# Input norm: weight and offset as rows spread by TensorE, first block's norm on VectorE alone, block 0 multiplied ahead of block 1's transposes

## Chip, core, metric

One core of a Trainium2 chip runs the whole program once. The metric is the device time of one execution in microseconds (us); several executions are summed up by their median. The engines are TensorE (PE, with its weight loads as PEld), VectorE (DVE), ScalarE (ACT), GpSimd (POOL) and SyncE (SP), which here only issues DMAs. Each engine runs its own program in order, and they wait for one another on semaphores.

## What is computed

One inference step of a decoder layer on 1024 prompt tokens and 64 sample tokens: an input layer norm, a combined projection that feeds sliding-window attention and a state-space mixer, an output projection, an MLP, and a gated embedding, each with a norm behind it. The change touches the start alone:

```
def layer_norm(x, g, b):
    mu = mean(x, -1); var = mean(square(x - mu), -1)
    return (x - mu) * rsqrt(var + LN_EPS) * g + b

hp, hs = layer_norm(x_prompt, ln_in_g, ln_in_b), layer_norm(x_sample, ln_in_g, ln_in_b)
...
proj = x @ w_in          # x is hp or hs: (tokens, 1024) @ (1024, 3080)
q, k, v, z, xbc, dt = split(proj)
...
```

## The kernel before

The tokens stand in NB = 9 blocks of 128 rows (the last has 64). In the function `stage_front` each block n passes through the same steps.

1. **Norm.** SP loads the block into X (three buffers). DVE's `statistics(n)` takes mean and variance (lines 109 to 112), POOL's `inverse_root(n)` makes 1/sqrt(var + eps) (lines 116, 118), DVE's `shift(n)` makes -mean/std (line 122), ACT's `normalise(n)` writes (x - mean)/std into H (line 127), POOL's `gain(n)` multiplies by the norm's weight G (line 132), and DVE's `add_bias(n)` adds the offset B (line 136) and raises `ln.done`. G and B are [128, 1024] tiles, each filled by a DMA that repeats one row of DRAM over 128 partitions.
2. **Transpose.** PE's `turn_x(n)` waits for `ln.done` and transposes the block in eight 128x128 pieces into PSUM (line 899; even blocks into fr_T, odd ones into fr_SS).
3. **Split.** ACT's `hi(n)` copies the transposed block to fp32r (line 732), DVE's `lo(n)` keeps the remainder (line 526). This pair stands in for an fp32 operand.
4. **Product.** PE's `tokens(n, 0)` multiplies the block by the first 344 columns of w_in for v and z: 24 matmuls (line 912; 8 pieces of the contraction times 3 hi/lo products). Those columns are split by ACT's `token_hi(0, k)` (line 736) and DVE's `token_lo(0, k)` (line 531), k = 0 to 7.

The order on each engine is written out by hand as a sequence of calls. On PE it is turn_x(0), turn_x(1), tokens(0), turn_x(2), tokens(1), turn_x(3), tokens(2), and so on: each product stands behind the transposes of the next block. On DVE add_bias(n + 1) stands behind lo(n), and on POOL inverse_root(n + 2) behind gain(n + 1). After the nine blocks come two more column groups of w_in and then 48 block products, all of which need every block's transposes; attention, projection and MLP follow as stages of their own.

Of the kernel before, what the change touches and what calls it, by code (L numbers as in the profile page):

```python
# [8 lines left out]
ALU = mybir.AluOpType  # L9
# [5 lines left out]
P = 128  # L15
# [143 lines left out]
def stage_front(nc, sem, io, ident, hT_hi, hT_lo, qT, kT, Xt, Bt, BT, CT, dt_raw, qk_start, xbc_start, top):  # L159
# [17 lines left out]
    X, H = norm("in_x", [P, 3, D]), norm("in_h", [P, 3, D])  # L177
    ln = LayerNorm(sem, norm, "in_ln")
    sb = lambda name, shape: top("sd_" + name, shape)
    tables = sb("tables", [P, sum(w for _, _, w in SSD_TABLES)])  # L180
    view, at = {}, 0
    for name, rows, width in SSD_TABLES:
# [27 lines left out]
             "xdt_done xdd_done masked e_done g_mm m_done y_mm o_mm off_done st_scaled y1_done s_mm st_done ss_low_scaled ss_high_scaled ss_done "  # L210
             "xsk_done y2_done y3_done z_loaded ssq_done ms_done rs_done yn_done st_out k_stored").split()
    S = {n: sem("fr_" + n) for n in names}
# [55 lines left out]
    with ExitStack() as ctx:  # L268
# [12 lines left out]
        def _(sp):  # L281
            def load_x(n):
                src = io["x_sample"] if n == NB - 1 else io["x_prompt"][n * P:(n + 1) * P, :]
                sp.dma_start(X[0:rows(n), n % 3, :], src).then_inc(x_loaded[n % 3], 16)
# [20 lines left out]

            load_x(0)
            sp.dma_start(ident[:, :], io["c_ident"]).then_inc(S["ident_loaded"], 16)
            sp.dma_start(ln.G[:, :], io["ln_in_g"].partition_broadcast(P)).then_inc(ln.loaded, 16)
            load_x(1)
            sp.dma_start(ln.B[:, :], io["ln_in_b"].partition_broadcast(P)).then_inc(ln.loaded, 16)  # L310
            load_token_weights(0)
# [100 lines left out]
        @block.gpsimd  # L412
        def _(pool):
            ln.constants(pool)

            def gain(n):
                r = rows(n)
                ln.gain(pool, H[0:r, n % 3, :], n % 2, n // 2, r)

            ln.inverse_root(pool, 0, 0, P)  # L420
            gain(0)
            ln.inverse_root(pool, 1, 0, P)
# [87 lines left out]
        def _(dve):  # L510
# [5 lines left out]
            def shift(n):  # L516
                ln.shift(dve, n % 2, n // 2, rows(n))

            def add_bias(n):
                ln.bias(dve, H[0:rows(n), n % 3, :], n % 2, n // 2, rows(n))  # L520
# [17 lines left out]
            statistics(0)  # L538
            shift(0)
            statistics(1)  # L540
            add_bias(0)
            shift(1)
            for k in range(KD // 2):
                token_lo(0, k)
            for n in range(NB):
                if n + 2 < NB:
                    statistics(n + 2)
                lo(n)
                if n == 0:
                    for k in range(KD // 2, KD):  # L550
                        token_lo(0, k)
                if n + 2 < NB:
                    shift(n + 2)
                if n + 1 < NB:
                    add_bias(n + 1)
# [165 lines left out]
        def _(act):  # L721
# [120 lines left out]

            normalise(0)
            for k in range(KD // 2):
                token_hi(0, k)
            normalise(1)
            for k in range(KD // 2, KD):
                token_hi(0, k)
            for n in range(NB):
                hi(n)  # L850
                if n + 2 < NB:
                    normalise(n + 2)
                if n >= 1:
                    evict_tokens(n - 1, 0)
                if 2 <= n < 6:
                    for k in range(2 * (n - 2), 2 * (n - 1)):
                        token_hi(1, k)
# [34 lines left out]
        def _(pe):  # L892
# [137 lines left out]

            pe.wait_ge(S["ident_loaded"], 16)
            turn_x(0)
            for n in range(NB):
                if n + 1 < NB:
                    turn_x(n + 1)
                tokens(n, 0)
# [1210 lines left out]
```

## Time and profile before

| what | value |
|---|---|
| median of 3 executions | 1626.64 us (1624.76 to 1627.03) |
| the profiled execution | 1625.73 us |
| its span, first to last instruction | 1623.9 us |
| PE busy | 1541.5 us, 95% of the span |
| DVE, ACT, POOL busy | 675.2, 489.1, 352.8 us |

The span is the time on the chip between the first and the last instruction that the trace shows; 1.8 us of the execution lie around it. Busy time says how long an engine had an instruction under way; matmuls overlap in their pipeline, so a busy PE need not be at its peak. Times in the trace's rows count from the start of the span.

### The profile page before, as it was taken

Reading aid. Unit: us, or ns where it says so; the run is one execution under the profiler, and the core shown is the slowest. Engines: PE = TensorE matmul, PEld = TensorE weight load, DVE = VectorE, ACT = ScalarE, POOL = GpSimd, SP = SyncE. Lnnn points to the kernel's source line nnn. Section 1 sums busy time; section 2 is a strip of 40 time slices with the busy share of each in tenths; the row PEclk is TensorE's granted clock in tenths of the full one; section 3 lists DMA queues with packets and bytes.
Section 4 is the critical chain, followed back from the end, with each engine's and each line's share of the span. In section 5 each row is a group of like instructions: output and inputs, shape, how many; then the busy total and the mean of one; then the engine's idle time right before and its main releaser. Section 6 shows DMA issues by size and latency. Waiting matters only on the chain.

```text
span 1623.9 us, 23323 instructions
## 1 busy us (share of the span) xinstructions
PE 1541.5 (95%) x9164; PEld 1343.1 (83%) x9164; DVE 675.2 (42%) x1233; ACT 489.1 (30%) x942; POOL 352.8 (22%) x375
## 2 busy tenths in 40 slices
PE   4999999998799989999999999999999999999997
PEld 4999998998365668798898989889898898977884
DVE  5412664552455655543232332323223232255655
ACT  4423223353456543342130302204021130323331
POOL 4300003463343522231010101101010010222442
PEclk9999999999899999999999999999999999999999
DMA  7531112441957221122030110202011020132011
GB/s 253 169 123 34 40 49 73 153 132 46 365 192 292 81 90 39 41 73 76 1 104 0 55 48 26 77 0 77 26 52 52 25 78 0 53 130 65 33 48 46
DMA packets 104655, 134.69 MB, mean 83 GB/s; under 512 B 6912, under 2 KB 78528, under 8 KB 104192
## 3 DMA queue, kind: packets, MB, share of 16 engines
q1 hardware_dynamic: 104576, 133.60, 24.6%
q8 instruction: 54, 0.88, 0.2%
q14 instruction: 25, 0.20, 0.0%
HBM read 113.25 MB, written 20.33 MB: 82 GB/s over the span
## 4 chain that ended last, share of the span: by engine, by line
PE 52%; issue 5%; DVE 3%; POOL 2%; DMA 1%; ACT 0%; SPq 0%; POOLq 0%; DVEq 0%; ACTq 0%
PE bk_U L1496 30%; PE bk_D L2016 18%; PE bk_D L1496 2%; POOL bk_u L1654 1%; PE bk_D L2011 1%; PE bk_D L2012 1%; DMA bk_wg_raw<-in_w_gate 1%; DVE bk_down_lo L1839 1%; DVE op_w_lo L1481 1%; DVE bk_m_lo L1823 1%; DVE R L1848 0%; PE bk_U L2048 0%; PE bk_D L1995 0%; POOL R L132 0%; DVE bk_wg_lo L1481 0%
## 5 line engine op out<-in xcount | busy, mean ns | idle before, releaser
L1496 PE MATMUL bk_U<-h1T_hi,bk_m_hi 128*128 128x364 f32 (+1 forms) x768 | 251.9, 328 | 4.8 <-PE bk_D L2016 4.8
L1496 PE MATMUL bk_U<-h1T_lo,bk_m_hi 128*128 128x364 f32 (+1 forms) x768 | 251.8, 328 | 0.0
L1496 PE MATMUL bk_U<-h1T_hi,bk_m_lo 128*128 128x364 f32 (+1 forms) x768 | 250.5, 326 | 0.0
L1654 POOL TENSOR_TENSOR bk_u<-bk_relu 128x364 f32<-128x364 f32 (+1 forms) x96 | 77.8, 811 | 639.9 <-ACT bk_relu L1701 639.8
L1701 ACT ACTIVATE bk_relu<-bk_U 128x364 f32<-128x364 f32 (+1 forms) x96 | 45.4, 473 | 554.4 <-PE bk_U L1496 554.4
L2016 PE MATMUL bk_D<-bk_down_hi,bk_u_hi 128*128 128x512 f32 x512 | 200.6, 392 | 6.5 <-DVE R L1848 3.1
L2016 PE MATMUL bk_D<-bk_down_lo,bk_u_hi 128*128 128x512 f32 x512 | 199.3, 389 | 0.0
L2016 PE MATMUL bk_D<-bk_down_hi,bk_u_lo 128*128 128x512 f32 x512 | 199.3, 389 | 0.0
L1848 DVE TENSOR_TENSOR R<-R,bk_D 128x512 f32<-128x512 f32 x144 | 98.5, 687 | 238.9 <-PE bk_D L2016 219.3
L1831 DVE TENSOR_TENSOR bk_u_lo<-bk_u,bk_u_hi 128x364 fp32r<-128x364 f32 (+1 forms) x96 | 50.9, 532 | 271.8 <-POOL bk_u L1654 271.8
L1496 PEld LDWEIGHTS bk_U<-h1T_hi,bk_m_hi 128*128 128x128 f32 x768 | 144.3, 188 | 7.8 <-issue 7.8
L1496 PEld LDWEIGHTS bk_U<-h1T_lo,bk_m_hi 128*128 128x128 f32 x768 | 144.4, 188 | 0.0
L1496 PEld LDWEIGHTS bk_U<-h1T_hi,bk_m_lo 128*128 128x128 f32 x768 | 144.1, 188 | 0.0
L923 PE MATMUL fr_mm<-hT_hi,fr_w_hi 128*128 128x364 f32 (+1 forms) x384 | 130.2, 339 | 0.0
L923 PE MATMUL fr_mm<-hT_hi,fr_w_lo 128*128 128x364 f32 (+1 forms) x384 | 126.5, 329 | 0.0
L923 PE MATMUL fr_mm<-hT_lo,fr_w_hi 128*128 128x364 f32 (+1 forms) x384 | 126.4, 329 | 0.0
L2016 PEld LDWEIGHTS bk_D<-bk_down_hi,bk_u_hi 128*128 128x128 f32 x512 | 96.1, 188 | 30.4 <-DVE bk_down_lo L1839 5.3
L2016 PEld LDWEIGHTS bk_D<-bk_down_hi,bk_u_lo 128*128 128x128 f32 x512 | 96.1, 188 | 20.1
L2016 PEld LDWEIGHTS bk_D<-bk_down_lo,bk_u_hi 128*128 128x128 f32 x512 | 96.1, 188 | 19.3
L1245 POOL TENSOR_TENSOR at_Z<-at_Z,at_inv 128x128 f32<-128x128 f32 (+7 forms) x64 | 72.1, 1147 | 101.8 <-DVE at_inv L1286 101.8
L923 PEld LDWEIGHTS fr_mm<-hT_hi,fr_w_hi 128*128 128x128 f32 x384 | 72.7, 189 | 1.1 <-issue 0.4
L923 PEld LDWEIGHTS fr_mm<-hT_lo,fr_w_hi 128*128 128x128 f32 x384 | 72.7, 189 | 0.2
(273 smaller groups left out, 2762.5 us busy)
## 6 DMA issues: line engine op xcount, KB each, us to landing
bk_up_raw<-in_w_up SPq DMA_DIRECT2D x32, 512.0 KB, 4.1
bk_down_raw<-in_w_down SPq DMA_DIRECT2D x32, 512.0 KB, 4.3
Kc<-in_cache_kT SPq DMA_DIRECT2D x8, 1536.0 KB, 13.5
Vc<-in_cache_v SPq DMA_DIRECT2D x8, 1536.0 KB, 9.8
fr_raw<-in_w_in SPq DMA_DIRECT2D x16, 512.0 KB, 4.0
in_x<-in_x_prompt SPq DMA_DIRECT2D x8, 512.0 KB, 6.2
h_scratch<-in_h SPq DMA_DIRECT2D x8, 512.0 KB, 3.2
sd_E<-acs_scratch SPq DMA_DIRECT2D x8, 512.0 KB, 3.8
```

What stands on the lines that cost most here:

```text
L923: last = pe.matmul(mm[:, u % 3, 0:w], wt[m % 2][:, k, :], ht[:, k, c:c + w], start=(k == 0 and part == 0), stop=(k == KD - 1 and part == 2))
L1245: pool.tensor_tensor(z, z, inv[:, m % NZ, u:u + 1].to_broadcast([P, n]), ALU.mult).then_inc(S["norm"], 1)
L1481: dve.tensor_tensor(self.lo[:, k, :], self.raw[:, k, :], self.hi[:, k, :].bitcast(F32), ALU.subtract).then_inc(self.lo_done, 1)
L1496: last = pe.matmul(out, a, b, start=(k == 0 and part == 0), stop=(k == n_k - 1 and part == 2))
L1654: pool.tensor_tensor(u[:, col:col + w], x, x, ALU.mult).then_inc(mul_done[g], 1)
L1701: act.activation(relu[:, col:col + w], pU[s][:, g, 0:w], ACT.Relu).then_inc(relu_done[s][g], 1)
L1823: dve.tensor_tensor(up_lo[s][:, :, :], up_raw[:, :, :], up_hi[s][:, :, :].bitcast(F32), ALU.subtract).then_inc(S["up_lo_done"], 1)
L1831: last = dve.tensor_tensor(u_lo[f][:, col:end], u[:, col:end], u_hi[f][:, col:end].bitcast(F32), ALU.subtract)
L1839: dve.tensor_tensor(down_lo[:, f, :], down_raw[:, :], down_hi[:, f, :].bitcast(F32), ALU.subtract).then_inc(S["down_lo_done"], 1)
L1848: dve.tensor_tensor(acc, acc, DD[:, s, :], ALU.add).then_inc(added[s], 1)
L2011: pe.matmul(out, both, down_hi[:, f, half], start=(f == 0), stop=False)
L2016: last = pe.matmul(out, a, b[:, f, half], start=(f == 0 and part == 0), stop=(f == FB - 1 and part == 2))
```

## The change

SP no longer fills G and B by DMA. It loads the two rows of 4 KB into partition 0 of H's third and second buffer (`g_row`, `b_row`), behind block 0 of X and ahead of `ident`. POOL sets a row of 128 ones. PE multiplies that row (as a 1x128 weight) with each half of the two rows, so that each of four matmuls with contraction 1 leaves 512 columns repeated over 128 partitions in PSUM, and ACT copies them to G and B.

Block 0's norm is `finish_first` on DVE: (x - mean) * G in one instruction and times 1/std plus B in a second, in place of shift, ACT's normalise, POOL's gain and add_bias. The order changes on PE (tokens(0) ahead of turn_x(1)), on ACT (hi(0) ahead of normalise(1)) and on DVE (below).

```diff
             load_x(0)
+            for row, src in ((g_row, io["ln_in_g"]), (b_row, io["ln_in_b"])):
+                sp.dma_start(row, src.rearrange("(a f) -> a f", a=1)).then_inc(S["rows_loaded"], 16)
             sp.dma_start(ident[:, :], io["c_ident"]).then_inc(S["ident_loaded"], 16)
-            sp.dma_start(ln.G[:, :], io["ln_in_g"].partition_broadcast(P)).then_inc(ln.loaded, 16)
             load_x(1)
-            sp.dma_start(ln.B[:, :], io["ln_in_b"].partition_broadcast(P)).then_inc(ln.loaded, 16)
...
             ln.inverse_root(pool, 0, 0, P)
-            gain(0)
             ln.inverse_root(pool, 1, 0, P)
...
+            def finish_first():
...
+                dve.wait_ge(ln.loaded, 32)
+                dve.wait_ge(ln.mv_done[0], 1)
+                dve.scalar_tensor_tensor(H[:, 0, :], X[:, 0, :], ln.mv[:, 0, 0:1], ln.G[:, :], ALU.subtract, ALU.mult)\
+                    .then_inc(ln.xn_done[0], 1)
+                dve.wait_ge(ln.xn_done[0], 1)
+                dve.wait_ge(ln.rstd_done[0], 1)
+                dve.scalar_tensor_tensor(H[:, 0, :], H[:, 0, :], ln.rstd[:, 0, :], ln.B[:, :], ALU.mult, ALU.add).then_inc(ln.done[0], 1)
...
             statistics(0)
-            shift(0)
+            finish_first()
             statistics(1)
-            add_bias(0)
             shift(1)
             for k in range(KD // 2):
                 token_lo(0, k)
-            for n in range(NB):
+            lo(0)
+            for k in range(KD // 2, KD):
+                token_lo(0, k)
+            add_bias(1)
+            statistics(2)
+            shift(2)
+            for n in range(1, NB):
...
-            normalise(0)
+            for v, (to, source) in enumerate(((ln.G, SS), (ln.B, mm))):
+                act.wait_ge(S["spread"], v + 1)
+                act.activation(to[:, :], source[:, 0:2, :].rearrange("p a b -> p (a b)"), ACT.Copy).then_inc(ln.loaded, 16)
...
             pe.wait_ge(S["ident_loaded"], 16)
+            pe.wait_ge(S["rows_loaded"], 32)
+            pe.wait_ge(S["one_set"], 1)
+            for to, row in ((SS, g_row), (mm, b_row)):
+                for half in range(2):
+                    last = pe.matmul(to[:, half, :], one[:, :], row[:, half * 512:(half + 1) * 512], start=True, stop=True)
+                last.then_inc(S["spread"], 1)
             turn_x(0)
-            for n in range(NB):
+            tokens(0, 0)
+            turn_x(1)
+            for n in range(1, NB):
                 if n + 1 < NB:
                     turn_x(n + 1)
                 tokens(n, 0)
```

On PE at the program's start, before (fr_T and fr_SS are the transposes' PSUM, fr_mm the products'; the seven further transposes of each block and, at the dots, block 0's further matmuls are left out):

```order
L899 MATMUL fr_T<-ident,in_h 128x128 [waits in_ln_done0,fr_ident_loaded]
L899 MATMUL fr_SS<-ident,in_h 128x128 [waits in_ln_done1]
L912 MATMUL fr_mm<-fr_t_hi_61,hT_hi 128x344 [waits fr_t_lo,fr_hT_lo_done]
...
L899 MATMUL fr_T<-ident,in_h 128x128 [waits fr_hT_lo_done,in_ln_done0]
L912 MATMUL fr_mm<-fr_t_hi_61,hT_hi 128x344 [waits fr_hT_lo_done]
```

And with the change, at the same place:

```order
L1057 MATMUL fr_SS<-in_h,in_one 128x512 [waits fr_one_set,fr_rows_loaded,fr_ident_loaded]
L1057 MATMUL fr_mm<-in_h,in_one 128x512 x2
L920 MATMUL fr_T<-ident,in_h 128x128 [waits in_ln_done0]
L933 MATMUL fr_mm<-fr_t_hi_61,hT_hi 128x344 [waits fr_t_lo,fr_hT_lo_done]
...
L920 MATMUL fr_SS<-ident,in_h 128x128 [waits in_ln_done1]
L920 MATMUL fr_T<-ident,in_h 128x128 [waits fr_hT_lo_done,in_ln_done0]
L933 MATMUL fr_mm<-fr_t_hi_61,hT_hi 128x344 [waits fr_hT_lo_done]
```

Block 0's product now stands between the transposes of blocks 0 and 1, and the transposes of block 2 follow at once on those of block 1.

On DVE, before, from the first split of the weights to block 2's offset:

```order
L531 TENSOR_TENSOR fr_t_lo_62<-fr_t_raw,fr_t_hi_61 128x344 [waits fr_t_hi_done] x4
L109 BN_STATS in_ln_bn<-in_x 128x6 [waits fr_x_loaded2]
...
L526 TENSOR_TENSOR hT_lo<-fr_T,hT_hi 128x8x128 [waits fr_hT_hi_done]
L531 TENSOR_TENSOR fr_t_lo_62<-fr_t_raw,fr_t_hi_61 128x344 [waits fr_t_hi_done] x4
L122 TENSOR_SCALAR in_ln_nmr<-in_ln_mv,in_ln_rstd 128x1 [waits in_ln_rstd_done0]
L136 TENSOR_TENSOR in_h<-in_h,in_ln_b 128x1024 [waits in_ln_gain_done1]
...
L526 TENSOR_TENSOR hT_lo<-fr_SS,hT_hi 128x8x128 [waits fr_hT_hi_done]
L122 TENSOR_SCALAR in_ln_nmr<-in_ln_mv,in_ln_rstd 128x1 [waits in_ln_rstd_done1]
L136 TENSOR_TENSOR in_h<-in_h,in_ln_b 128x1024 [waits in_ln_gain_done0]
```

And with the change:

```order
L546 TENSOR_TENSOR fr_t_lo_62<-fr_t_raw,fr_t_hi_61 128x344 [waits fr_t_hi_done] x4
L541 TENSOR_TENSOR hT_lo<-fr_T,hT_hi 128x8x128 [waits fr_hT_hi_done]
L546 TENSOR_TENSOR fr_t_lo_62<-fr_t_raw,fr_t_hi_61 128x344 [waits fr_t_hi_done] x4
L136 TENSOR_TENSOR in_h<-in_h,in_ln_b 128x1024 [waits in_ln_gain_done1]
L109 BN_STATS in_ln_bn<-in_x 128x6 [waits fr_x_loaded2]
...
L122 TENSOR_SCALAR in_ln_nmr<-in_ln_mv,in_ln_rstd 128x1 [waits in_ln_rstd_done0]
...
L541 TENSOR_TENSOR hT_lo<-fr_SS,hT_hi 128x8x128 [waits fr_hT_hi_done]
L122 TENSOR_SCALAR in_ln_nmr<-in_ln_mv,in_ln_rstd 128x1 [waits in_ln_rstd_done1]
L136 TENSOR_TENSOR in_h<-in_h,in_ln_b 128x1024 [waits in_ln_gain_done0]
```

Block 2's statistics have moved from ahead of block 0's split to behind block 1's offset.

On ACT the program now begins with these rows; before, the load of the activation table waited for nothing:

```order
L862 ACT_TABLE_LOAD [waits fr_spread]
L862 ACTIVATE in_ln_g<-fr_SS 128x1024
L862 ACTIVATE in_ln_b<-fr_mm 128x1024 [waits fr_spread]
L753 ACTIVATE fr_t_hi_61<-fr_t_raw 128x344 [waits fr_t_loaded0] x4
L749 ACTIVATE hT_hi<-fr_T 128x8x128 [waits fr_x_turned]
L127 ACTIVATE in_h<-in_x,in_ln_nmr,in_ln_rstd 128x1024 [waits in_ln_nmr_done1]
```

The table load has moved behind the first pair of spreading matmuls.

## Rows read from the trace of the kernel before

**Rows 1.** The page's first part: busy us, share of span, instructions.

```profile
PE 1541.5 (95%) x9164; PEld 1343.1 (83%) x9164; DVE 675.2 (42%) x1233; ACT 489.1 (30%) x942; POOL 352.8 (22%) x375
```

**Rows 2.** Windows: us; PE, PEld, DVE, ACT, POOL busy (instructions); granted clock; DMA share, GB/s.

```profile
0.00:16.00 16.00, 0.28 (x2) 0.31 (x3) 4.55 (x10) 4.15 (x6) 4.99 (x11) 1.00 0.79 282
71.00:76.00 5.00, 5.00 (x34) 5.00 (x33) 0.00 (x0) 1.91 (x3) 0.00 (x0) 1.00 1.05 305
```

**Rows 3.** Timeline, 0 to 16 us: start, us, instruction, [idle before <- releaser].

```profile
0.73 1.28 ACT L127 ACT_TABLE_LOAD   x1 [0.73 <-PEq L2235]
2.12 0.43 SPq L284 DMA_DIRECT2D in_x<-in_x_prompt  x1
4.32 0.69 DVE L109 BATCH_NORM_STATS2 in_ln_bn<-in_x 128x6 f32<-128x512 f32 x1 [4.32 <-DMA in_x<-in_x_prompt]
5.71 0.20 DVE L112 BATCH_NORM_AGGREGATE in_ln_mv<-in_ln_bn 128x2 f32<-128x12 f32 x1
6.91 0.21 DVE L122 TENSOR_SCALAR in_ln_nmr<-in_ln_mv,in_ln_rstd 128x1 f32<-128x1 f32 x1 [1.00 <-POOL in_ln_rstd L118]
11.97 2.34 POOL L132 TENSOR_TENSOR in_h<-in_h,in_ln_g 128x1024 f32<-128x1024 f32 x1 [5.10 <-DMA in_ln_b<-in_ln_in_b]
15.72 1.94 PE L899 MATMUL fr_T<-ident,in_h 128*128 128x128 f32 x8 [15.72 <-DVE in_h L136]
```

**Rows 4.** DMA issues, 0 to 20 us: KB each, median us to landing.

```profile
in_ln_g<-in_ln_in_g SPq DMA_DIRECT2D x1, 512.0 KB, 7.1
ident<-in_c_ident SPq DMA_DIRECT2D x1, 64.0 KB, 3.3
```

**Rows 5.** Timeline of PE, 24 to 36 us: transposes of blocks 1 to 3, block 0's first matmul.

```profile
24.20 1.97 PE L899 MATMUL fr_SS<-ident,in_h 128*128 128x128 f32 x8 [6.54 <-DVE in_h L136]
25.82 0.64 PE L912 MATMUL fr_mm<-fr_t_hi,hT_hi 128*128 128x344 f32 x1
31.10 1.03 PE L899 MATMUL fr_T<-ident,in_h 128*128 128x128 f32 x8
35.76 1.09 PE L899 MATMUL fr_SS<-ident,in_h 128*128 128x128 f32 x8
```

**Rows 6.** Timeline of DVE, ACT, POOL, 21 to 29 us: steps of blocks 1 and 2.

```profile
21.11 1.79 DVE L531 TENSOR_TENSOR fr_t_lo<-fr_t_raw,fr_t_hi 128x344 fp32r<-128x344 f32 x4
23.05 1.24 ACT L127 ACTIVATE in_h<-in_x,in_ln_nmr,in_ln_rstd 128x1024 f32<-128x1024 f32 x1 [3.12 <-DVE in_ln_nmr L122]
24.44 2.36 POOL L132 TENSOR_TENSOR in_h<-in_h,in_ln_g 128x1024 f32<-128x1024 f32 x1 [3.52 <-ACT in_h L127]
26.21 1.02 ACT L732 ACTIVATE hT_hi<-fr_SS 128x1024 fp32r<-128x1024 f32 x1 [1.91 <-PE fr_SS L899]
27.02 0.55 POOL L118 TENSOR_TENSOR in_ln_rstd<-in_ln_veps,in_ln_mhalf 128x1 f32<-128x1 f32 x1
27.27 1.23 DVE L526 TENSOR_TENSOR hT_lo<-fr_SS,hT_hi 128x1024 fp32r<-128x1024 f32 x1 [1.62 <-ACT hT_hi L732]
28.53 1.22 DVE L136 TENSOR_TENSOR in_h<-in_h,in_ln_b 128x1024 f32<-128x1024 f32 x1
```

**Rows 7.** Timeline of PE, later: plain fp32 matmuls of 256 columns, contraction 128 and 32.

```profile
292.52 1.08 PE L1006 MATMUL fr_SS<-sd_state,CT 128*128 128x256 f32 x4
277.71 6.09 PEld L1022 LDWEIGHTS fr_SS<-sd_xdd,sd_Bz 32*128 32x128 f32 x16 [0.39 <-DVE sd_state_s L676]
```

**Rows 8.** Groups by line on DVE, 1600 to 1624 us: last block's norm, first instruction.

```profile
L1927 DVE SCALAR_TENSOR_TENSOR bk_gate<-bk_gate,bk_ln_mv,bk_ln_g 64x1024 f32<-64x1024 f32 x1 | 1.3, 1270 | 0.0
```

**Rows 9.** Windows where the granted clock changes: columns as in rows 2.

```profile
397.50:398.00 0.50, 0.26 (x3) 0.02 (x1) 0.00 (x0) 0.50 (x2) 0.00 (x0) 1.00 0.00 0
401.00:401.50 0.50, 0.00 (x0) 0.00 (x0) 0.00 (x0) 0.00 (x0) 0.00 (x0) 0.52 1.06 386
278.00:279.00 1.00, 1.00 (x4) 0.79 (x4) 0.52 (x1) 0.00 (x0) 1.00 (x1) 0.57 0.00 1
280.00:281.00 1.00, 1.00 (x4) 0.76 (x3) 0.20 (x1) 0.00 (x0) 0.00 (x0) 0.50 0.00 0
```

More of the change, by code:

```diff
@@ L178, in stage_front @@
     ln = LayerNorm(sem, norm, "in_ln")
+    one = norm("in_one", [1, P])
+    g_row, b_row = H[0:1, 2, :], H[0:1, 1, :]
     sb = lambda name, shape: top("sd_" + name, shape)
@@ L210, in stage_front @@
              "xdt_done xdd_done masked e_done g_mm m_done y_mm o_mm off_done st_scaled y1_done s_mm st_done ss_low_scaled ss_high_scaled ss_done "
-             "xsk_done y2_done y3_done z_loaded ssq_done ms_done rs_done yn_done st_out k_stored").split()
+             "rows_loaded one_set spread xsk_done y2_done y3_done z_loaded ssq_done ms_done rs_done yn_done st_out k_stored").split()
     S = {n: sem("fr_" + n) for n in names}
@@ L413, in _ @@
         def _(pool):
+            pool.memset(one[:, :], 1.0).then_inc(S["one_set"], 1)
             ln.constants(pool)
@@ L517, in shift @@
                 ln.shift(dve, n % 2, n // 2, rows(n))
+            def finish_first():
[6 more added lines that the diff above has]
+                dve.scalar_tensor_tensor(H[:, 0, :], H[:, 0, :], ln.rstd[:, 0, :], ln.B[:, :], ALU.mult, ALU.add).then_inc(ln.done[0], 1)
+                dve.sem_inc(ln.nmr_done[0], 1)
+                dve.sem_inc(ln.gain_done[0], 1)
             def add_bias(n):
@@ L548, in _ @@
                 lo(n)
-                if n == 0:
-                    for k in range(KD // 2, KD):
-                        token_lo(0, k)
                 if n + 2 < NB:
@@ L841, in read_turned @@
                 last.then_inc(S["uev"], 1)
-            normalise(0)
+            for v, (to, source) in enumerate(((ln.G, SS), (ln.B, mm))):
+                act.wait_ge(S["spread"], v + 1)
+                act.activation(to[:, :], source[:, 0:2, :].rearrange("p a b -> p (a b)"), ACT.Copy).then_inc(ln.loaded, 16)
             for k in range(KD // 2):
                 token_hi(0, k)
+            hi(0)
             normalise(1)
@@ L849, in _ @@
             for n in range(NB):
-                hi(n)
+                if n >= 1:
+                    hi(n)
                 if n + 2 < NB:
```

## The prediction, made blind

> **What bounds the kernel now.** I read the page's busy shares first, then the windows of the start, then the timeline of each engine there. The shares say that PE is the engine to look at: busy 95% of the span [rows 1]. The windows say where it is not: in the first 16 us PE works 0.28 us, and from some point on it works without a gap (5.00 of 5 us at 71 us) [rows 2]. In between, PE begins block 0's transposes at 15.72 us, block 1's at 24.20, block 0's product at 25.82 [rows 3, 5], and the rest follows closely. So the front is worth what it moves PE's later work. I measure that at one point: the start of block 3's transposes, 35.76 us [rows 5]. In both programs PE has by then done the transposes of blocks 0 to 2 and the products of blocks 0 and 1, and what follows has the same order.
>
> What holds the first 15.72 us? Block 0's statistics begin when X lands, at 4.32, and end at 5.91; 1/std is there 1.00 us later [rows 3]. Then POOL's gain sits idle 5.10 us, until 11.97, for the landing of B, which is a DMA of 512 KB; gain takes 2.34 and the offset 1.2 more [rows 3, 6]. That wait is what the change goes after. The second idle stretch, up to 24.20, ends with block 1's offset on DVE [rows 5].
>
> **Part 1: when block 0's norm is done (T0).** The rows of G and B are small, and `ident`, which PE also waits for, is now fourth in SP's queue, where X of block 1 was issued at 2.12; with its 3.3 us to land it is there at 5.4 [rows 3, 4]. Bounds: 4.5 if it lands as early as before (two places earlier in the queue, which takes some 0.45 us a place), 8.8 if the second row, issued where G was (about 1.65), takes the 7.1 us that G took [rows 4]. I take 5.4: a row of 4 KB is nearer to ident's 64 KB than to G's 512.
>
> No row shows a matmul with contraction 1 and 512 columns in fp32. The nearest are fp32 with 256 columns: four in 1.08 us at contraction 128, 0.27 each, and 16 weight loads (one to a matmul) in 6.09 us at contraction 32, 0.38 each, the latter while the granted clock stood at 0.50 [rows 7, 9]. PE comes out of idleness here, and block 0's and 1's transposes (1.94, 1.97) take twice those of blocks 2 and 3 (1.03, 1.09) [rows 3, 5], so I price at the half clock: 512 columns between 2 x 0.38 = 0.76 and 4 x 0.27 = 1.08; I take 0.85, nearer to the row of small contraction. The first pair ends at 5.4 + 1.7 + 0.2 of pipeline = 7.3, the second at 9.0.
>
> ACT's table load takes 1.28 us; before it ran at 0.73, under the load of X [rows 3], and now the first pair's wait stands ahead of it, so that cover is gone: 8.6. Each copy out of PSUM is priced as ACT's 1.02 for the same size [rows 6]: G at 9.65, B at 10.7. The two DVE instructions of `finish_first` are like the last block's, 1.27 each [rows 8]: T0 = 13.3. Before, it was 15.7, PE's start. So this part gives 2.4 us. Bounds from the above: 12.1 (all low) to 16.7 (rows landing at 8.8).
>
> The Trainium skill, page "FP8 and Floating Point Precision", section "TensorE Precision Notes", says that true fp32 takes four passes through the array. The trace does not bear it out: 0.27 us for 256 columns is 2.5 times the 0.107 of one pass at 2.4 GHz. By the page each spreading matmul would cost about 1.7 us, the second pair would end at 12.4, and T0 would be 16.0.
>
> Costed at nothing: 1 MB less to load (X of block 1 and the weights come earlier, but DVE reads block 1 only after T0, and ACT the weights after the copies), POOL's memset of 128 ones (it ends under the load of X), POOL's gain of block 0 (POOL has nothing else to do then). The load of X for block 3 now waits for `finish_first`'s first half, at 12; its reader comes at T0 + 11 = 24, and 7 us to land [rows 4] fit.
>
> **Part 2: from T0 to block 2's offset.** Here DVE's order is the matter. After T0 one chain runs through DVE, POOL and ACT, each step priced from a row: block 1's statistics 1.6, 1/std 1.0, shift 0.1 [rows 3]; four weight splits at 1.7 (they start to start in 1.79 less overlap), block 0's `lo` 1.2, four more splits 1.7, block 1's offset 1.15 [rows 6]: T0 + 8.5. Only then block 2's statistics, 1/std and shift, 2.7: T0 + 11.2. Then ACT's normalise 1.24 and POOL's gain and, queued behind gain, block 3's 1/std: in the trace from 23.05 to 27.57, 4.5 us [rows 6]. DVE's shift of block 3 waits for that 1/std, and block 2's offset (1.22) stands behind the shift: T0 + 17.2.
>
> PE in that time: transposes of block 0 at T0, product at T0 + 5.7 = 19.0, when `lo` is done. Before, that product ran from 25.82 to 31.10, 5.28 us [rows 5]; now until 24.3, and block 1's transposes until some 25.5 to 26.5. Block 1's own path (ACT's hi 1.02, lo 1.23) ends before POOL's chain and costs nothing. But PE's next instruction is block 2's transposes, at T0 + 17.2 = 30.5. Nothing stands between: **PE waits 4 to 5 us**, where before block 0's product filled that place. So the product starts 6.8 us earlier and most of it is given back in one stall; block 2's transposes start at 30.5 against 31.10 [rows 5].
>
> **Part 3: the clock.** Out of a warm stretch, block 2's transposes and block 1's product take 35.76 - 31.10 = 4.66 us; the same work out of idleness took 31.10 - 24.20 = 6.90 (blocks 1 and 0) [rows 5]. So 2.24 us hang on whether the granted clock falls from 2.4 to 1.2 GHz in the stall. PE's last work before attention is at 397.8, and the clock falls between 401.0 and 401.5; it also falls in a stretch of matmuls with contraction 32, at which PE is busy throughout [rows 9]. A stall of 4 to 5 us is longer than those 3.5, so I take the fall as likelier. The windows give a clock of 1.00 for the first 16 us too [rows 2], where the transposes take the time of the half clock; at the start I go by the durations.
>
> The Trainium skill, page "TensorE: Matmul & The Clock Gate", section "HAM oscillation — how this bites in real kernels", speaks against this change: idle gaps between groups of matmuls put the clock back, and each group starts slow. By that rule the stall costs its idle time and the 2.24 us.
>
> **Sum.** 30.5 + 6.90 = 37.4 against 35.76: +1.6 us. On the profiled execution's 1625.73 that is 1627.4. The median of the runs shown is 0.9 above that execution; I add half of it: **1627.8 us**.
>
> **Rivals.**
> - *The clock holds through the stall* (PE stopped for less than at 397.8, or the fall comes too late to matter): 30.5 + 4.66 = 35.2, -0.6: 1625.1. For it: the fall at 401 took 3.5 us of full idleness, and the stall may be shorter.
> - *The spread is late* (slower). The rows land as late as G did, which puts T0 at 16.7, or the spreading matmuls take twice the time priced, which puts it at 16.0. Everything hangs on T0, so the point moves by 2.7 to 3.4 more: +4.3 to +5.0, 1630.0 to 1630.7. It decides from T0 = 14.9 on (+3.25 in all). Against it: ident's 3.3 us and the rows of 256 columns.
> - *The stall does not come* (faster): block 2's offset is ready when PE wants it, PE goes on from block 0's product at 24.3 through block 1's transposes (1.03) and 4.66 more: 30.0, -5.8: 1619.9. For it: PE's first product does start 6.8 us earlier. Against it: the order of DVE and POOL, by which block 2's statistics come after block 1's offset; all 17.2 us of the chain are priced from rows, and 6 us of them would have to vanish.
> - *Nothing moves:* would need T0 at 13.9 with the clock held, or near 11.7 with the fall; it lies inside the range.
>
> **Numbers.** About 0.2%, 3.25 us, is what a measurement of this kernel can tell from no change. The forecast has 0.55, the clock that holds 0.25; both lie within 0.2%. The late spread has 0.13 (slower; 0.08 by late rows, 0.05 by dear matmuls), the missing stall 0.07 (faster). The range leaves these last two out: low 1625.1 less the 1.2 of T0's low bound, 1623.9; high 1627.4 with T0 at 14.9 (+1.6) and the whole 0.9 of the median, 1629.9.
>
> **What would show it.** Right: G's copy waiting for a table load after the first spread; the second instruction of `finish_first` ending near 13.3; block 0's product starting near 19; PE idle 4 to 5 us before block 2's transposes with DVE's offset as releaser, and block 2's transposes at 1.9 us rather than 1.0 behind it; block 3's transposes at 37.4. Wrong: T0 beyond 15 (rows or spreading matmuls dearer than priced), no stall there, or a difference that arises after 40 us, where I expect none.

## The result, and the profile after

| | before | after |
|---|---|---|
| median of 11 executions each, us | 1627.03 (1624.41 to 1629.83) | 1633.01 (1630.11 to 1634.1) |
| ratio of the times | | 1.0034, 95% interval 1.0026 to 1.0042 |
| the profiled execution, us | 1625.73 | 1633.81 |
| block 0's transposes start | 15.72 | 16.25 |
| block 2's transposes start | 31.10 | 34.32 |
| block 3's transposes start | 35.76 | 40.56 |
| block 8's transposes start (the last) | 60.22 | 65.04 |

The kernel is slower by 0.34%, some 6 us. The prediction said 1627.8 us, no change that can be told (0.80), slower with 0.13; the time lies outside its range, 1623.9 to 1629.9. First the top of the page, against [rows 1]:

```profile
span 1632.0 us, 23348 instructions
...
PE 1553.9 (95%) x9172; PEld 1349.9 (83%) x9172; DVE 677.6 (42%) x1233; ACT 489.4 (30%) x943; POOL 349.8 (21%) x375
```

PE is busy 12.4 us longer; the eight records of the spread are 7.2 us of that (5.24 to 12.43). The timeline of the changed kernel up to 17 us answers to [rows 3]:

```profile
5.24 3.78 PE L1057 MATMUL fr_SS<-in_h,in_one 1*128 1x512 f32 x4 [5.24 <-DMA ident<-in_c_ident]
...
8.81 3.62 PE L1057 MATMUL fr_mm<-in_h,in_one 1*128 1x512 f32 x4
9.10 1.28 ACT L862 ACT_TABLE_LOAD   x1 [9.10 <-PE fr_SS L1057]
10.40 1.02 ACT L862 ACTIVATE in_ln_g<-fr_SS 128x1024 f32<-128x1024 f32 x1
12.53 1.02 ACT L862 ACTIVATE in_ln_b<-fr_mm 128x1024 f32<-128x1024 f32 x1 [1.11 <-PE fr_mm L1057]
...
13.59 1.28 DVE L526 SCALAR_TENSOR_TENSOR in_h<-in_x,in_ln_mv,in_ln_g 128x1024 f32<-128x1024 f32 x1 [7.51 <-ACT in_ln_b L862]
...
14.91 1.28 DVE L530 SCALAR_TENSOR_TENSOR in_h<-in_h,in_ln_rstd,in_ln_b 128x1024 f32<-128x1024 f32 x1
```

The rows and `ident` are there at 5.24, as forecast. But the program issues two spreading matmuls for a row, and the trace has four records for it (x4), 0.85 us each: the first row is spread at 9.1, the second at 12.4. The table load, the copies and the two DVE instructions follow at their forecast lengths, and block 0's norm is done at 16.2.

PE from there on, against [rows 5]:

```profile
16.25 1.97 PE L920 MATMUL fr_T<-ident,in_h 128*128 128x128 f32 x8 [3.82 <-DVE in_h L530]
21.73 0.66 PE L933 MATMUL fr_mm<-fr_t_hi,hT_hi 128*128 128x344 f32 x1 [3.52 <-DVE hT_lo L541]
...
28.15 1.04 PE L920 MATMUL fr_SS<-ident,in_h 128*128 128x128 f32 x8
...
34.32 1.97 PE L920 MATMUL fr_T<-ident,in_h 128*128 128x128 f32 x8 [5.13 <-DVE in_h L136]
...
40.56 1.03 PE L920 MATMUL fr_SS<-ident,in_h 128*128 128x128 f32 x8
```

Block 0's product does start early (21.73 against 25.82), and PE then stands 5.13 us for block 2's offset. Block 3's transposes are 4.80 late, block 8's 4.82: from there on nothing is won back or lost in the front.

The windows of the changed kernel (us; busy of PE, PEld, DVE, ACT, POOL; granted clock) at the stall and in the tail:

```profile
33.50:34.00 0.50, 0.00 (x0) 0.00 (x0) 0.50 (x1) 0.50 (x1) 0.00 (x0) 1.00 0.05 16
34.00:34.50 0.50, 0.18 (x1) 0.19 (x2) 0.50 (x2) 0.50 (x2) 0.00 (x0) 0.68 0.00 0
34.50:37.50 3.00, 3.00 (x13) 3.00 (x13) 1.35 (x5) 1.35 (x2) 2.79 (x3) 0.50 0.83 266
...
1454.00:1458.00 4.00, 4.00 (x12) 3.13 (x11) 1.16 (x2) 3.95 (x4) 2.39 (x1) 0.57 0.00 0
...
1488.00:1492.00 4.00, 4.00 (x12) 3.17 (x11) 1.52 (x2) 2.31 (x3) 0.00 (x0) 0.57 0.99 320
```

Before, at the same times (the same work lies 5 to 7 us earlier there, where the clock reads 1.00 too):

```profile
1452.00:1458.00 6.00, 6.00 (x28) 4.96 (x27) 3.93 (x8) 1.02 (x2) 1.24 (x3) 1.00 0.00 0
1488.00:1492.00 4.00, 4.00 (x19) 3.24 (x18) 0.00 (x0) 0.00 (x0) 0.00 (x0) 1.00 0.07 20
```

And PE's first matmuls behind its two pauses in that part of the tail, before (the first two) and after:

```profile
1448.27 0.50 PE L2016 MATMUL bk_D<-bk_down_hi,bk_u_hi 128*128 128x512 f32 x1 [1.81 <-DVE R L1848]
1481.09 0.47 PE L1496 MATMUL bk_U<-bk_wg_hi,bk_m_hi 128*128 128x512 f32 x1 [3.14 <-DVE bk_wg_lo L1481]
...
1453.20 0.50 PE L2045 MATMUL bk_D<-bk_down_hi,bk_u_hi 128*128 128x512 f32 x1 [1.81 <-DVE R L1877]
1487.64 0.47 PE L1525 MATMUL bk_U<-bk_wg_hi,bk_m_hi 128*128 128x512 f32 x1 [3.14 <-DVE bk_wg_lo L1510]
```

The granted clock falls to 1.2 GHz (0.50) as PE comes out of the stall. In the tail it falls twice more, behind pauses of PE of 1.81 and 3.14 us; before has the same two pauses, and its clock stays at 1.00. These two falls make the difference of the two spans 8.1 us instead of 4.8 to 5.1. They come and go from one execution to the next: of the 14 profiles of this case, 6 have the first fall (after, e2, e3, e6, e9, e10) and 13 the second, all but this first one of before (see `before_again` below). So I read a kernel's front at block 8's transposes, and its time from the medians.

### The profile page after: what moved, and what is told of

Its sections match the earlier page's. It is cut to its first block, busy times and chain, and to the rows that moved or that the text cites. A ratio compares the mean times of both kernels' runs of the same rounds, so it can differ in the third digit from the quotient of the medians.

```text
span 1632.0 us, 23348 instructions
## 1 busy us (share of the span) xinstructions
PE 1553.9 (95%) x9172; PEld 1349.9 (83%) x9172; DVE 677.6 (42%) x1233; ACT 489.4 (30%) x943; POOL 349.8 (21%) x375
## 4 chain that ended last, share of the span: by engine, by line
PE 52%; issue 5%; DVE 3%; POOL 2%; DMA 1%; ACT 0%; SPq 0%; POOLq 0%; DVEq 0%; ACTq 0%
PE bk_U L1525 30%; PE bk_D L2045 18%; PE bk_D L1525 2%; POOL bk_u L1683 1%; PE bk_D L2040 1%; PE bk_D L2041 1%; DMA bk_wg_raw<-in_w_gate 1%; DVE bk_down_lo L1868 1%; DVE op_w_lo L1510 1%; DVE bk_m_lo L1852 1%; DVE R L1877 0%; PE bk_U L2077 0%; PE bk_D L2024 0%; POOL R L132 0%; DVE bk_wg_lo L1510 0%
## 5 line engine op out<-in xcount | busy, mean ns | idle before, releaser
L933 PE MATMUL fr_mm<-fr_t_hi,hT_hi 128*128 128x344 f32 (+1 forms) x216 | 71.3, 330 | 3.5 <-DVE hT_lo L541 3.5
## 6 DMA issues: line engine op xcount, KB each, us to landing
Kc<-in_cache_kT SPq DMA_DIRECT2D x8, 1536.0 KB, 13.3
```

Of the source, the lines that this page charges most:

```text
L933: last = pe.matmul(mm[0:r, u % 3, 0:TOKEN_GROUP], ht[:, k, to], wt[g][:, k, :], start=(k == 0 and part == 0), stop=(k == KD - 1 and part = ...
```

## The experiments

Starts of PE's transposes, us, from one profile each. T0 is the start of block 0's.

| kernel | T0 | block 2 | block 3 | block 8 | block 8 against before | ratio of times (95%) |
|---|---|---|---|---|---|---|
| before | 15.72 | 31.10 | 35.76 | 60.22 | | |
| after | 16.25 | 34.32 | 40.56 | 65.04 | +4.82 | 1.0034 (1.0026 to 1.0042) |
| e1_norm_only | 15.82 | 32.54 | 37.21 | 61.71 | +1.49 | 1.0020 (1.0011 to 1.0030) |
| e2_order_only | 15.48 | 33.52 | 39.52 | 63.99 | +3.77 | 1.0035 (1.0021 to 1.0049) |
| e5_half_spread | 13.20 | 31.25 | 38.13 | 62.55 | +2.33 | 1.0026 (1.0015 to 1.0037) |
| e3_psum_direct | 13.37 | 31.90 | 38.37 | 62.80 | +2.58 | 1.0024 (1.0015 to 1.0033) |
| e9_no_gain1 | 16.43 | 33.31 | 39.55 | 64.01 | +3.79 | one execution |
| e4_stats2_early | 15.78 | 29.13 | 37.84 | 63.68 | +3.46 | 1.0025 (1.0014 to 1.0035) |
| e6_block1_early | 13.99 | 31.18 | 36.09 | 60.54 | +0.32 | 1.0005 (0.9995 to 1.0014) |
| e8_norm_old_loads | 14.71 | 30.06 | 34.72 | 59.18 | -1.04 | 0.9995 (0.9986 to 1.0004) |
| e10_norms_first | 12.46 | 26.79 | 32.60 | 61.62 | +1.40 | 1.0025 (1.0016 to 1.0035) |
| e11_spread_norms_first | 13.55 | 27.12 | 32.93 | 61.95 | +1.73 | 1.0027 (1.0017 to 1.0036) |
| e12_norms_first_old_loop | 13.25 | 28.46 | 33.37 | 57.83 | -2.39 | 0.9981 (0.9972 to 0.9990) |

**The two parts apart: e1_norm_only and e2_order_only.** e1 puts before's order back into the changed kernel, but for one thing: `finish_first` still stands ahead of block 1's statistics on DVE. e2 puts the new order alone into before.

```diff
 e1, PE, against after (DVE and ACT likewise; e2, against before, the reverse)
             turn_x(0)
-            tokens(0, 0)
-            turn_x(1)
-            for n in range(1, NB):
+            for n in range(NB):
```

> The changed kernel with the order of before on VectorE, ScalarE and TensorE; the rows, their spread by TensorE and the two instructions of finish_first stay. Theory A (the loss is the dear spread plus the order): block 0's norm is done at 16.2 as in the changed kernel (15.7 before), block 1's statistics come behind it, so block 1's transposes start near 26.8 (24.20 before), block 2's near 33.7 (31.10), block 3's near 38.4 (35.76), with no stall over 1 us ahead of block 2's transposes and the clock held from there on; the whole is 2.6 us slower than before and some 2 us faster than the changed kernel. Rival B (the loss arises after 40 us, in stages where the clock falls): the total does not follow block 3's transposes, and this kernel is as slow as the changed one (+5.5 us) though its point is 2 us earlier.

> The kernel before with its loads and its norm of block 0 left as they are (shift, normalise, gain, offset), and only the new order of instructions on VectorE, ScalarE and TensorE. Theory A: block 0's norm is done at 15.7 as before; block 1's statistics are out of the way by then, so block 2's offset comes at some 32.5 (16.8 behind block 0's); TensorE stands idle for 5 to 6 us between block 1's and block 2's transposes, the granted clock falls to about 0.5 there, and block 3's transposes start 6.2 later, near 38.7: +2.9 against before, with nothing of the spread in it. Rival C (the order is harmless, the whole loss is the spread's lateness): block 3's transposes at 35.8 or earlier, no stall, and the time as before within 1 us.

e1's block 8 is +1.49, e2's +3.77; together 5.26, about the changed kernel's 4.82. Both parts lose, and the order loses more, without any spread in it. e1's T0 is within 0.1 us of before's; what it loses comes behind T0. Block 1's statistics, which before has done by 12.2, start at 15.68, behind `finish_first`, and block 1's transposes start at 26.38 instead of 24.20. In e2 PE:

```profile
24.98 1.09 PE L904 MATMUL fr_SS<-ident,in_h 128*128 128x128 f32 x8
33.52 1.97 PE L904 MATMUL fr_T<-ident,in_h 128*128 128x128 f32 x8 [7.45 <-DVE in_h L136]
```

The wait for block 2's offset is 7.45 us, longer than forecast: T0 to block 2 took 18.0, not 16.8. Rival C (the order is harmless) falls. Rival B (the whole loss arises after 40 us) falls with e1: its time is between the two kernels', as its front is. That nothing is lost after 40 us does not follow: e2's time is some 5.7 us above before's (1.0035), its front 3.77.

**Was the matmul's price the wrong step? e5_half_spread and e3_psum_direct.** e5 issues one matmul for a row (ACT's copy puts that half into both), and its spread then costs what I had priced. e3 leaves out the wait for ACT's table load and copies instead.

```diff
 e5
-                for half in range(2):
-                    last = pe.matmul(to[:, half, :], one[:, :], row[:, half * 512:(half + 1) * 512], ...)
+                last = pe.matmul(to[:, 0, :], one[:, :], row[:, 0:512], ...)
 e3, finish_first (offset likewise, from mm)
-                dve.wait_ge(ln.loaded, 32)
+                dve.wait_ge(S["spread"], 1)
-                ... ln.mv[:, 0, 0:1], ln.G[:, :], ALU.subtract, ALU.mult)
+                ... ln.mv[:, 0, 0:1], flat_pair(SS), ALU.subtract, ALU.mult)
```

> The changed kernel with one spreading matmul for each row in place of two: only the first 512 numbers of weight and offset are spread, and the copy puts them into both halves, so the columns from 512 on get other weights and offsets than the reference's. One matmul (two records of 0.85) then takes what the prediction priced for two. Theory A (the price of the spreading matmul is the step of the sum that failed, the rest of the sum stands): the first spread is done near 7.2, block 0's norm at 13.3, block 2's transposes at 30.5 to 31.4, block 3's at 37.4 (prediction) to 37.7, and the time 1.6 to 2 us above before. Rival (block 0's norm is held by something else, the landing of the rows or X, not by the spread): block 0's norm at 16, block 3's transposes at 40.5 as in the changed kernel.

> The changed kernel, but the two instructions of finish_first read weight and offset straight from PSUM; ScalarE copies them out for the later blocks only after VectorE has read them. Theory A (the spread holds block 0's norm, and what follows is a chain of fixed length behind it): the second spread is done at 12.3, so block 0's norm at 13.6 to 13.9 (16.2 in the changed kernel), block 2's transposes 18.1 later, near 31.9, with a stall of 5 to 6 us ahead of them; block 8's transposes near 62.7 (65.04 in the changed kernel, 60.22 before); the time 2.5 to 4 us above before. Rival (an instruction that reads PSUM is dearer, or the later copies hold ScalarE's weight splits up, so that nothing is won): block 8's transposes at 64 or later.

e5's timeline:

```profile
5.11 2.07 PE L1056 MATMUL fr_SS<-in_h,in_one 1*128 1x512 f32 x2 [5.11 <-DMA ident<-in_c_ident]
...
13.20 1.97 PE L920 MATMUL fr_T<-ident,in_h 128*128 128x128 f32 x8 [4.31 <-DVE in_h L530]
...
31.25 1.97 PE L920 MATMUL fr_T<-ident,in_h 128*128 128x128 f32 x8 [6.05 <-DVE in_h L136]
...
38.13 1.03 PE L920 MATMUL fr_SS<-ident,in_h 128*128 128x128 f32 x8
```

One matmul, two records (x2). With the price that I had assumed, block 0's norm is done at 13.2 (prediction 13.3), block 3's transposes start at 38.1 (37.4), and the kernel is still slower than before. The 0.7 that is left at block 3 lies between T0 and block 2 (18.05 instead of 17.2; next experiment). The time misses its forecast of 1.6 to 2 us above before: it is some 4.2 us above (1.0026), the front 2.33. e3 comes within 0.3 us of its forecast at each start (13.37, 31.90, 62.80), though its stall is 6.71, not 5 to 6. So the spread's price shifts T0, what follows shifts with it, and the stall came at every T0 measured with this order (13.20 to 16.43).

**The shared wait of VectorE and GpSimd: e9_no_gain1.** The chain from T0 to block 2's transposes took 18.1 us in the changed kernel, not 17.2. Its timeline:

```profile
18.75 1.79 DVE L546 TENSOR_TENSOR fr_t_lo<-fr_t_raw,fr_t_hi 128x344 fp32r<-128x344 f32 x4
...
20.55 2.36 POOL L132 TENSOR_TENSOR in_h<-in_h,in_ln_g 128x1024 f32<-128x1024 f32 x1 [1.96 <-ACT in_h L127]
21.59 2.97 DVE L546 TENSOR_TENSOR fr_t_lo<-fr_t_raw,fr_t_hi 128x344 fp32r<-128x344 f32 x4
24.49 1.21 DVE L136 TENSOR_TENSOR in_h<-in_h,in_ln_b 128x1024 f32<-128x1024 f32 x1
```

The second group of four weight splits takes 2.97 where the first takes 1.79, and runs beside POOL's gain. e9 leaves out that gain:

```diff
             def gain(n):
+                if n == 1:
+                    ...
+                    pool.sem_inc(ln.gain_done[1], 1)
+                    return
```

> The changed kernel without GpSimd's gain of block 1 (its rows leave the norm without the weight). Theory D (the 2.97 us that the second group of weight splits takes, 1.2 more than the first, is time in which VectorE stands while GpSimd's gain runs): that group takes 1.8, block 1's offset starts near 23.3 instead of 24.49, block 2's transposes 1.2 earlier, near 33.1, block 8's near 63.9. Rival (the group waits for ScalarE's splits or for something else): it still takes 3 us, and block 2's transposes stay at 34.3.

e9's rows of the same steps:

```profile
21.77 1.79 DVE L551 TENSOR_TENSOR fr_t_lo<-fr_t_raw,fr_t_hi 128x344 fp32r<-128x344 f32 x4
23.47 1.22 DVE L136 TENSOR_TENSOR in_h<-in_h,in_ln_b 128x1024 f32<-128x1024 f32 x1
```

The group takes 1.79 again, and the chain is 16.9 (33.31 - 16.43), 1.2 less. So DVE stood while the gain ran.

**Taking the stall away: e4_stats2_early.** Block 2's norm is started earlier (on POOL its 1/std goes ahead of block 1's gain):

```diff
 e4, DVE, against after
             statistics(1)
+            statistics(2)
             shift(1)
 ...
             lo(0)
+            shift(2)
 ...
             add_bias(1)
-            statistics(2)
-            shift(2)
+            add_bias(2)
```

> The changed kernel with block 2's statistics right behind block 1's, its 1/std ahead of block 1's gain on GpSimd, its shift behind block 0's lo and its offset right behind block 1's offset. Theory A: block 0's norm is done at 16.2 as in the changed kernel, block 2's offset is done before TensorE has finished block 1's transposes, so the stall of 5.1 us is gone or under 1.5 us, the clock does not fall, and block 3's transposes start near 36.1 (40.56 in the changed kernel, 35.76 before): the time is that of before within 1 us, 4 to 5 us less than the changed kernel's. Rival B (the loss arises after 40 us): the time stays about 5 us above before. Rival D (VectorE and GpSimd hold each other up at SBUF, so that earlier work of block 2 only takes longer): single instructions of 1.7 to 2.4 us instead of 0.5 to 1.2 on VectorE while GpSimd's gain runs, and block 3's transposes after 38.

The stall ahead of block 2 is gone, as forecast, but 36.1 for block 3 was missed by 1.7, and the front is still +3.46. The time was forecast within 1 us of before's and is some 4 us above it (1.0025). e4's timeline:

```profile
21.63 4.90 DVE L547 TENSOR_TENSOR fr_t_lo<-fr_t_raw,fr_t_hi 128x344 fp32r<-128x344 f32 x4
...
29.13 1.04 PE L922 MATMUL fr_T<-ident,in_h 128*128 128x128 f32 x8
31.66 0.43 PE L935 MATMUL fr_mm<-fr_t_hi,hT_hi 128*128 128x344 f32 x1 [1.50 <-DVE hT_lo L542]
...
37.84 1.93 PE L922 MATMUL fr_SS<-ident,in_h 128*128 128x128 f32 x8 [2.12 <-DVE in_h L136]
```

Two gains now run beside the splits, which take 4.90 us; all later steps of DVE slide, and PE waits in two other places, for lo of block 1 and for block 3's offset (2.12, at which the clock falls: 1.93 us for the transposes). Rival D had the larger part of this. A stall taken away at one block came back, shorter, at the next.

**Better orders: e8, e6, e10, e11, e12.** e8 keeps before's loads and order and takes only the norm on VectorE, behind block 1's statistics; e6 spreads the rows as e3 does and moves block 1's norm ahead of the end of block 0's, with before's order on PE (the diff shows the main lines; ACT's copies and normalise move in e6 too).

```diff
 e8, DVE, against before
             statistics(0)
-            shift(0)
             statistics(1)
-            add_bias(0)
+            finish_first()
             shift(1)
 e6, DVE, against after
             statistics(0)
-            finish_first()
             statistics(1)
             shift(1)
+            finish_first()
+            statistics(2)
             ...
```

> The kernel before with one part of the change alone: block 0's norm on VectorE by finish_first, behind block 1's statistics; weight and offset are loaded spread out by DMA as before, and every order is that of before. Theory A: the landing of the offset (11.97 before) still releases it, but two VectorE instructions (2.5 us) follow in place of gain and offset (3.7), so block 0's norm is done near 14.6 (15.6 before), 1/std of block 1 is no longer queued behind block 0's gain, block 1's transposes start near 23.0 (24.20), block 3's near 34.6 (35.76), block 8's near 59.0 (60.22): 1 to 1.5 us faster than before. Rival (the norm on VectorE is itself a loss, since VectorE is the engine that every block waits for): block 8's transposes at 60.2 or later.

> Rows, spread and finish_first from PSUM as in e3_psum_direct, TensorE's order as before (block 1's transposes ahead of block 0's product), and block 1's statistics, 1/std, shift and normalise put ahead of block 0's end, into the time in which the spread is awaited; block 2's statistics come right behind finish_first. Theory A (what counts is the chain of norms on VectorE, GpSimd and ScalarE, and the wait for the spread is room for block 1's part of it): block 0's norm is done at 13.9, block 1's near 18.5, TensorE has block 0's product from 20.5 on, no stall over 1 us ahead of block 2's transposes, block 3's transposes between 30.4 and 32 (35.76 before) and block 8's near 55 to 56.5 (60.22 before): 4 to 5 us faster than before. Rival D (VectorE's instructions with two SBUF inputs stand while GpSimd's gain runs): the weight splits take 3 to 5 us a group instead of 1.8, block 3's transposes at 33 to 34, 2 us faster at most.

e8's front came as forecast at each point (14.71, 23.20, 34.72, 59.18): with DMA-spread rows the norm on VectorE gains 1.04 us. That is too little for the times to show (0.9995). In e6 the splits stood beside a gain once more (3.67 us), and that gain waited until 17.08 for ACT's copy of the offset. Its forecast failed: block 1's transposes start at 22.27 (18.5 forecast), block 3's at 36.09 (30.4 to 32, and 33 to 34 by rival D), and it is as fast as before instead of 4 to 5 us faster.

e10 splits finish_first, so that its first half waits for the weight alone, and puts all norm steps ahead of the weight splits; e11 is the same with the spread of e3.

```diff
             statistics(0)
+            finish_first()       # (x - mean) * G
             statistics(1)
+            finish_second()      # * 1/std + B
             shift(1)
+            statistics(2)
+            lo(0)
+            add_bias(1)
+            shift(2)
             (8 splits)
             for n in range(1, NB):
                 statistics(n + 2)
-                lo(n)
-                shift(n + 2)
                 add_bias(n + 1)
+                shift(n + 2)
+                lo(n)
```

> The loads of before; block 0's norm on VectorE as in e8_norm_old_loads, but its first instruction waits for the weight alone and goes ahead of block 1's statistics; behind it VectorE and ScalarE do what the next norms wait for first (statistics of block 2, offset of block 1, shift of block 2), and the weight splits after that; later blocks take the offset ahead of the lo of the block before. TensorE's order is that of before. Theory A and D together (the chain of norms sets the front; weight splits beside a running gain only stand): block 0's norm is done near 13.4, block 1's transposes start near 19, block 0's product near 21 with no stall over 1 us behind it, block 3's transposes near 32.2 (35.76 before), block 8's near 56.6 (60.22): 3 to 4 us faster than before. Rival (the norms are not the bound, VectorE's whole work is): block 8's transposes at 59 as in e8_norm_old_loads, or later, with VectorE busy without a gap from 14 to 30.

> The same order with the rows spread by TensorE and read from PSUM as in e3_psum_direct. Theory A: the second spread is done at 12.3, where the offset of before lands at 12.0, so block 0's norm is done near 13.5, as in e10_norms_first; ScalarE's copies for the later blocks put block 1's gain 0.6 to 1 us later, and block 8's transposes come within 1 us behind those of e10_norms_first, near 57.2, 3 us ahead of before. Rival (the rows are worth something that the order hid): 1 us or more ahead of e10_norms_first. Rival (the copies cost ScalarE what the weight splits and hi of block 0 need): 2 us or more behind it.

Up to block 3 e10 is where it was forecast (32.60, 3.2 ahead of before). Then it loses 0.88 us at each block, 5.81 where before takes 4.93. Its DVE:

```profile
32.98 0.21 DVE L122 TENSOR_SCALAR in_ln_nmr<-in_ln_mv,in_ln_rstd 128x1 f32<-128x1 f32 x1 [0.43 <-POOL in_ln_rstd L118]
33.11 1.21 DVE L542 TENSOR_TENSOR hT_lo<-fr_T,hT_hi 128x1024 fp32r<-128x1024 f32 x1
```

lo(2) stands behind a shift that waits for POOL, while PE, done with block 3's transposes (32.60), waits for lo(2), 0.69 us at each block. My loop, not the idea, was wrong. The rival's number (59 or later) came true, its reason did not: DVE is busy 12.8 of the 16 us from 14 to 30. e11 runs 0.33 us behind e10 from block 2 on, as forecast; spread or loaded rows come to the same within the 0.8 us by which the landing of the weight differs between two executions (below). Its block 8 fails with e10's loop. e12 puts the loop of before back:

```diff
                 statistics(n + 2)
+                lo(n)
+                shift(n + 2)
                 add_bias(n + 1)
-                shift(n + 2)
-                lo(n)
```

> e10_norms_first with one thing put back: from block 1 on, VectorE takes lo of the block ahead of the shift and the offset of the next ones, as the kernel before does. Theory A, with what e10_norms_first showed (its front was early, block 3's transposes at 32.60, but each later block took 5.81 us instead of 4.93, because lo stood behind a shift that waits for 1/std): block 2's transposes start near 27.6, block 3's near 32.4 and each block behind takes 4.93 us again, so block 8's start near 57.0 (60.22 before) and the time is some 3 us below that of before, a ratio near 0.998. Rival (the early front leaves block 3 or 4 without its norm, and a stall of 2 to 4 us comes there): block 8's transposes at 59 or later, as in e8_norm_old_loads.

e12's PE:

```profile
13.25 1.94 PE L915 MATMUL fr_T<-ident,in_h 128*128 128x128 f32 x8 [13.25 <-DVE in_h L531]
20.53 1.97 PE L915 MATMUL fr_SS<-ident,in_h 128*128 128x128 f32 x8 [5.34 <-DVE in_h L136]
28.46 1.10 PE L915 MATMUL fr_T<-ident,in_h 128*128 128x128 f32 x8 [0.72 <-DVE in_h L136]
33.37 1.09 PE L915 MATMUL fr_SS<-ident,in_h 128*128 128x128 f32 x8
```

Stall 0.72, blocks 4.9 apart again, block 8 at 57.83. All points lie 0.8 to 1.0 behind those forecast: in this execution the weight landed at 9.07, in e10's at 8.26, and T0 moved with it. The median is 1624.58 against 1628.10 in the same comparison: 0.9981 (0.9972 to 0.9990), faster than both kernels. That is 3.5 us for a front of 2.39; where the rest comes from is not shown, and the profiled execution (1627.82) is the slowest of its eleven.

**The tail: before_again**, the kernel before unchanged.

> The kernel before, unchanged, profiled once more. If the two short falls of the granted clock near 1450 and 1485 us, which the changed kernel's execution shows and the first one of before does not, belong to the execution and not to the change, an execution of before can show one or both as well, and is then 1.5 to 3 us longer than the first (span 1623.9) with the same front (block 3's transposes at 35.8, block 8's at 60.2). If they come of the change, this execution has none and its span is within 0.5 us of 1623.9.

Its front is 0.38 us earlier than in the first profile, its span 2.5 longer, and it has a window of which the first profile has none like it:

```profile
1480.00:1486.00 6.00, 3.97 (x11) 3.15 (x12) 2.85 (x3) 2.05 (x3) 0.00 (x0) 0.72 0.99 309
```

So the second fall belongs to the execution and not to the change. The first one is in 6 profiles of 14, e6's among them, whose front is within 0.4 us of before's; that it too comes by execution is likely, but no kernel was profiled both with it and without.

## Why the prediction was wrong, point by point

- **Rows and `ident` at 5.4:** right (5.24). Rival "late rows" did not happen.
- **The price of a spreading matmul, 0.85:** this is the step that failed, and T0 at 16.25 is beyond the 15 that I named as a sign of it. I read [rows 7]'s "x4 in 1.08" as four matmuls. The program has 16 matmuls on that line; the trace of before answers for it, over the whole span:

```profile
L1006 PE MATMUL fr_SS<-sd_state,CT x32: 379/379/435, 292.5 to 383.7; 128*128 128x256 f32 x32
...
L1022 PEld LDWEIGHTS fr_SS<-sd_xdd,sd_Bz x32: 181/185/332, 273.8 to 283.5; 32*128 32x128 f32 x32
```

Thirty-two records, two for each matmul, and as many weight loads for the 16 matmuls of line 1022: by the same reckoning 256 columns cost 0.54 us, not 0.27, and the bounds for 512 columns were 1.52 to 2.16 us, twice my 0.76 to 1.08. A spreading matmul takes 2 x 0.855 = 1.71 us, between them: the reckoning was right, its unit wrong. Of T0's 2.9 us too much (16.2 for 13.3), 1.8 come with the first row and the rest with the second, whose copy waits for it (1.11 us of idleness in ACT's row). The rival "matmuls twice the price" (T0 16.0, point 4.3 late) is what happened in the front; I gave it 0.05. Its time, 1630.0, is still 3 us short.
  The Trainium skill, page "FP8 and Floating Point Precision", section "TensorE Precision Notes", has true fp32 in four passes, and I wrote that the trace did not bear it out. With two records to a matmul it does: by that page 4 x 512 columns at 1.2 GHz are an estimated 1.71 us, which is the measured figure. How the passes lie in the records no run here shows.
- **Table load in front of the first copy, copies 1.02, DVE 1.27 each:** right (1.28, 1.02, 1.28). e3 shows what ACT's part costs: from the landing of `ident` to T0 it takes 8.57 us (13.37 - 4.80), the changed kernel 11.01 (16.25 - 5.24).
- **T0 to block 2's offset, 17.2:** measured 18.1; 1.2 of it is DVE standing beside POOL's gain (e9), which I had not looked for; the other steps came out a little shorter.
  The Trainium skill, page "SBUF — State Buffer", section "SBUF: two separate sides", says that a VectorE instruction with two SBUF inputs and a GpSimd instruction that reads SBUF share a port pair, which the one that starts first holds for its whole instruction. The rows agree: of the four splits beside the gain one took 1.69 us, the others 0.50, while lo, which reads PSUM and SBUF, took its 1.22 beside the same gain.
- **A stall of 4 to 5 us ahead of block 2, released by the offset:** right (5.13), in e2 without the rest of the change too. Its size is in part luck: the chain to the offset was 0.9 us longer than forecast, and block 0's product took 6.42 us (21.73 to 28.15), not 5.28.
- **The clock falls there:** right (0.50 from 34.5 to 37.5). Transposes and product took 6.24 us against 6.90 forecast: here the matmuls are at full speed again from 37.6 on, 3.3 us behind the start; in the stretch before from which I took the 6.90 they are from 28.8 on, 4.6 us behind it.
- **Nothing after 40 us:** right for the front (4.80 at block 3, 4.82 at block 8), wrong for the time. Of the 5.2 us from 1627.8 to 1633.01, 3.2 are the front (4.80 for 1.6). Another 0.85 is the start of the sum: I took before as 1626.2, between its profiled execution and its median of three, and its median is 1627.03 here; that execution is the one profile of 14 without a fall in the tail. The last 1.2 (6.0 between the medians, 4.8 in the front) arise behind the front and were not in my sum.
  Two things there differ from profile to profile. One is the falls in the tail. The other is a stretch at 1.2 GHz near 280 us: the mean granted clock from 270 to 295 us is 0.80 in both profiles of before, in after, e2, e3 and e8, 0.86 in e5 and e6, and 0.73 in the others; against before, PE wins some 1.5 us there at 0.86 and loses 1.1 to 1.4 at 0.73 (so e10, 1.96 us behind before when it gets there, is 3.3 behind in attention). Whether a late front makes either likelier, or chance did, stays open.

The sum with the one price put right, T0 16.2 and the rest of the prediction as it stands, gives block 3 at 40.3; measured 40.56. That it comes so close is in part luck: the chain behind T0 was 0.9 us too short in it, transposes and product 0.7 too long. The time by it would be 1627.8 + 2.9 = 1630.7, already beyond the range; the rest to 1633.01 is the 0.85 and the 1.2 above, and 0.3 of the front.

## What to carry to other kernels

Count a line's records against the program's instructions before dividing a row's time by its count: here one plain fp32 matmul is two records, while a transpose or an fp32r matmul is one. When an order is changed so that a wait is filled, follow the freed engine to its next wait: here a product moved ahead left nothing to cover the next block's norm, and e4 shows that pulling one block's norm forward can move the stall to the next. What paid (e12) was to put every step that another engine waits for ahead of the splits that only VectorE and TensorE need, at the start alone, and to leave the steady loop as it was.

## What of the hardware was not expected

- A matmul with contraction 1 and 512 fp32 columns takes 1.71 us here, at the start of the program. The transposes behind it take 1.97 us a block, against 1.03 later: the time of the half clock, though the windows print a granted clock of 1.00 there ([rows 2] for before).
- VectorE and GpSimd hold each other up in both directions: in e10 eight splits took their normal 3.50 us and POOL's gain beside them 4.25 in place of 2.35, ending 2.3 us behind the last of them:

```profile
19.72 3.50 DVE L547 TENSOR_TENSOR fr_t_lo<-fr_t_raw,fr_t_hi 128x344 fp32r<-128x344 f32 x8
...
21.23 4.25 POOL L132 TENSOR_TENSOR in_h<-in_h,in_ln_g 128x1024 f32<-128x1024 f32 x1 [2.88 <-ACT in_h L127]
```

- The granted clock falls in the tail in some executions of one and the same program and not in others, some 1.5 us for each fall (2.8 in e12's profile), behind a pause of PE that is the same length where it does not fall.
